# A hybrid decoder layer on one core: TensorE's unrolled recurrence heads written as a hardware loop

## The reference

```python
h = rms_norm(x, g_pre_mix)
z = h @ w_in                       # 16464 columns: q,k,v, indexer, HGRN q,f,i,g and two merge gates
o_a = sparse attention over the top-k keys
# HGRN2, 16 heads of 128 x 128
f = lb + (1 - lb) * sigmoid(hf);  k = 1 - f
b = cumsum(log f)                  # within a chunk
o = (q*exp(b)) @ S + causal((q exp(b)) . (k exp(-b))) @ v
S = exp(b_end) * S + (k * exp(b_end - b)).T @ v
o_b = rms_norm(o) * silu(hg)
x = x + rms_norm((sigmoid(ga)*o_a + sigmoid(gb)*o_b) @ w_out)
x = x + rms_norm(cross_attend(rms_norm(x), memory))
x = x + rms_norm(conv_ffn(rms_norm(x)))
```

## Time and profile before

| | us |
|---|---|
| median of 3 runs | 2759.55 |
| lowest, highest | 2756.3, 2761.29 |
| profiled execution, its own time | 2759.55 |
| its span, first to last instruction | 2758.0 |
| outside the span | 1.55 |
| a turn of two heads in the HGRN stage | 97.64 |

### The profile page before, as it was taken

The page is one execution under the profiler, slowest core; times in us unless marked ns, Lnnn a source line. Parts: engine busy times, 40 slices in busy tenths (PEclk is TensorE's granted clock), DMA queues, the critical chain, the costliest instruction groups (busy, mean ns, idle before and its releaser), DMA issues.

```text
span 2758.0 us, 49470 instructions
## 1 busy us (share of the span) xinstructions
PE 2693.2 (98%) x20086; PEld 2558.8 (93%) x20086; DVE 1605.0 (58%) x2399; ACT 1081.5 (39%) x1363; POOL 200.0 (7%) x293
## 2 busy tenths in 40 slices
PE   8999999999999999999989999999999999999998
PEld 7999787799999999999889969989999999999997
DVE  5564564376777768777446334475655555653334
ACT  5332444444444444444434234443322333333334
POOL 0103211011111111111000000000000000000000
PEclk9999999999999999999999999999999999999999
DMA  9646656765655555555464694555555555445554
GB/s 295 175 123 165 207 170 200 218 187 148 161 150 159 152 148 155 147 156 153 125 204 123 212 391 115 142 161 148 145 149 152 152 147 145 140 136 149 154 147 145
DMA packets 693458, 458.59 MB, mean 166 GB/s; under 512 B 13646, under 2 KB 661422, under 8 KB 687342
## 3 DMA queue, kind: packets, MB, share of 16 engines
q1 hardware_dynamic: 681008, 414.25, 52.9%
q0 software_dynamic: 8608, 28.06, 3.6%
q10 hardware_dynamic: 3712, 14.35, 1.4%
HBM read 429.91 MB, written 26.72 MB: 166 GB/s over the span
## 4 chain that ended last, share of the span: by engine, by line
PE 92%; DVE 4%; ACT 2%; DMA 1%; issue 1%; ACTq 0%; POOL 0%; POOLq 0%; DVEq 0%; SPq 0%
PE psum L595 20%; PE psum L600 20%; PE psum L597 20%; PE psum L840 4%; PE psum L1264 4%; PE psum L1265 4%; PE psum L1266 4%; PE psum L845 2%; PE psum L983 1%; PE psum L986 1%; PE psum L979 1%; PE psum L1144 1%; PE psum L701 1%; DMA ring<-in_w_in 1%; PE psum L995 1%
## 5 line engine op out<-in xcount | busy, mean ns | idle before, releaser
L595 PE MATMUL psum<-x_high,w_high 128*128 128x320 f32 x3808 | 1131.3, 312 | 4.2 <-ACT w_high L1987 4.0
L597 PE MATMUL psum<-h_low,w_high 128*128 128x320 f32 x3344 | 985.0, 309 | 0.0
L1311 DVE TENSOR_TENSOR w_low<-ring,w_high 128x2048 fp32r<-128x2048 f32 x292 | 676.2, 2316 | 321.7 <-ACT w_high L1987 321.3
L1987 ACT ACTIVATE w_high<-ring 128x2048 fp32r<-128x2048 f32 x294 | 561.8, 1912 | 724.7 <-PE psum L600 555.7
L595 PEld LDWEIGHTS psum<-x_high,w_high 128*128 128x128 f32 x3808 | 715.4, 188 | 9.3 <-ACT w_high L1987 4.8
L597 PEld LDWEIGHTS psum<-h_low,w_high 128*128 128x128 f32 x3344 | 629.0, 188 | 2.7 <-issue 1.0
L600 PE MATMUL psum<-x_high,w_low 128*128 128x320 f32 x3808 | 597.4, 309 | 0.0
L600 PEld LDWEIGHTS psum<-x_high,w_low 128*128 128x128 f32 x3808 | 568.5, 188 | 0.0
L1264 PE MATMUL psum<-y_high,w_down_high 128*128 128x320 f32 x704 | 217.8, 309 | 3.3 <-DVE w_low L1907 1.7
L1266 PE MATMUL psum<-y_high,w_low 128*128 128x320 f32 x704 | 216.3, 307 | 0.0
L1265 PE MATMUL psum<-y_low,w_down_high 128*128 128x320 f32 x704 | 216.2, 307 | 0.0
(11 more groups left out here) (425 smaller groups left out, 2838.9 us busy)
## 6 DMA issues: line engine op xcount, KB each, us to landing
ring<-in_w_in SPq DMA_DIRECT2D x128, 1024.0 KB, 5.8
ring<-in_w_up SPq DMA_DIRECT2D x88, 1024.0 KB, 5.7
ring<-in_w_down SPq DMA_DIRECT2D x64, 704.0 KB, 4.7
ring<-in_w_xk SPq DMA_DIRECT2D x16, 1024.0 KB, 6.1
ring<-in_w_xv SPq DMA_DIRECT2D x16, 1024.0 KB, 5.2
ring<-in_w_out SPq DMA_DIRECT2D x16, 1024.0 KB, 5.8
ring<-in_w_xq SPq DMA_DIRECT2D x16, 1024.0 KB, 5.9
ring<-in_w_xo SPq DMA_DIRECT2D x16, 1024.0 KB, 5.8
```

The lines of the kernel that those rows point to most:

```text
L595: mm(out, w_hi[:, j % 2, k, :], x_hi[:, k, :], start=k == 0, stop=False)
L597: mm(out, w_hi[:, j % 2, k, :], lo[:, k, :], start=False, stop=False)
L1311: V.tensor_tensor(w_lo[:, j], ring[:, j], w_hi[:, j % 2].bitcast(FP32), ALU.subtract).then_inc(N.slab_lo, 1)
L1987: F(w_hi[:, j % 2], ring[:, j], ACT.Copy).then_inc(N.slab_hi, 1)
```

## The change

On PE alone, the Python loop that wrote out seven pairs of heads becomes a hardware loop of seven turns. The last two heads stay written out.

```diff
             by_chunks(B_HG, 1, h_lo, lambda q: pe.wait_ge(rows_loaded[q], 32), lambda q: None)
-            for it in range(NHG // 2 - 1):
+            with pe.Fori(0, NHG // 2 - 1) as it:
                 head(it, 0)
                 head(it, 1)
             head(NHG // 2 - 1, 0)
             head(NHG // 2 - 1, 1, last_head=True)
```

## The result

The changed kernel takes 2790.7 us (median of 4 runs, 2786.5 to 2795.4) against 2758.3 us for the kernel before on the same chip. The ratio is 1.0114, with a 95% interval of 1.0095 to 1.0134. The prediction had the sign and the place right. It had the size wrong: it said 2771, and the time lies just above its range, in the rival "two misses at each jump".

What follows compares the result with a forecast made beforehand. The prediction took PE, busy in all of the stage, as the bound. It summed 2759.55 - 0 (copies removed) + 1.4 (register work) + 10.2 (six jumps) = 2771.2, said 2771, range 2757 to 2789.

Steps and rivals of the forecast that it cites:

- two misses at each jump: Rival at the loop's jumps: the top's block and the next both fetched, 28 to 46 us, 2789 to 2807; chance 0.17.
- PE bounds the stage, and a pause adds one for one: In the heads' stage PE is busy all 97.64 us of a turn, so any unfed moment adds to the end.
- Removing the copies is worth nothing: Dropping six of seven body copies on PE gains 0, as the 51 code packets held up nothing.
- Register work, 1.4 us: Register operations for turn-dependent waits in the loop's body: 0.1 us a head, 1.4 us in all, bounds 0 to 4.
- The rival that exposed it in full, 4 us: Rival in the loop's body: register work fully exposed, 4 us, with a miss of 1.9 us, 2775; no chance of its own.
- The first block is gone at each of the six jumps: At each jump back, the body's first block has left PE's instruction memory and must be fetched; size 10.2 us over six.
- 1.7 us a jump: Idle PE at each jump back: 4.1 us until PE is fed less 2.4 us of queued matmuls; 0 to 1.9 by bounds.
- No loss of clock: After a pause of 1.7 us at a jump PE keeps full clock; beyond about 2.9 it would add 3 us a jump.
- One miss a jump, 0.61, against two, 0.17: Likeliest case at the loop's jumps: one block fetched at each, 2762 to 2780, chance 0.61; fetching two had 0.17.
- The rival of a resident body: Rival at the jumps: the whole body stays in PE's instruction memory, only register work is left, 2761; chance 0.2.
- faster: Rival in the stage: fewer code fetches free DMA time for weight tiles, at most 3 us, giving 2757; chance 0.02.

Runs made afterwards that it cites:

- e5_hint_top: The changed kernel with a prefetch hint for the backward branch as the first instruction of each turn: 2760.7 us against 2757.9, ratio 1.0006.
- e2_half: The changed kernel with three loops of two turns in place of one of seven, the seventh pair written out: 2768.7 us against 2759.0, ratio 1.0031.
- e8: The kernel before, with four groups of four tiles in a turn of the FFN up loop (L1123), top at place 0 of a block: 2761.0 us, ratio 1.0006.
- e9: The kernel before, with four groups of four tiles in a turn of the FFN up loop, top at place 230 of a block: 2790.2 us, ratio 1.0111.
- e11_up5: The kernel before, with five groups of four tiles in a turn of the FFN up loop, top at place 0 of a block: 2763.6 us, ratio 1.0023.
- e4_slot239: The changed kernel with the loop's first instruction at place 239 of a block of 256: 2807.1 us against 2759.0, ratio 1.0165.
- e3_slot0: The changed kernel with the loop's first instruction at the first place of a block of 256: 2783.6 us against 2759.0, ratio 1.0079.

## Why the prediction was right or wrong, point by point

- *PE bounds the stage, and a pause adds one for one.* Right. The busy columns of DVE and ACT are as before, and pauses, restarts and clock make up the turns' growth.
- *Removing the copies is worth nothing.* Right (e5_hint_top: one copy, no miss, and the pace of before). It removed no fetches either: 67 packets came in the stage where 51 had the earlier trace rows.
- *Register work, 1.4 us.* It is nothing that can be seen: where e2_half has no jump, its pace is that of before. The rival that exposed it in full, 4 us, fell with it.
- *The first block is gone at each of the six jumps.* Right, and right that ten blocks would be needed. e8 and e9 now show why: eight stay, one of them fetched ahead. By the Trainium skill, Runtime: NRT & Kernel Launch, section Instruction fetch mechanics, PE holds 2048 instructions; the trace of e8_up4 agrees with eight blocks, but e11_up5 and e9_up4_slot230 (1972 and 1578 instructions) jump with a miss, so a body below 2048 is no safe sign.
- *1.7 us a jump.* This is the first term that was mis-sized. The fetch with its branch was put at 3.8 us. At the third and fifth jump that is what it took, 3.8 and 3.9 us, with pauses of 1.93 and 1.96. At the other four it took 4.8 to 4.9 us, with pauses of 2.9 to 3.0: there the block's packet waited behind POOL's store of a head's state (the table below), and the bounds from single DMAs allowed for no other traffic. The six first pauses are 15.6 us, not 10.2.
- *No loss of clock.* Wrong, a term put at nothing. The clock fell to 1.2 GHz behind four of six jumps, which cost 1.4 to 1.5 us each (a busy column of 99.67 where 98.14 stands without it). The reading of the earlier trace rows, a loss after 2.9 us and none after 1.6, does not carry over: the pauses ahead of the falls were 1.93, 2.87, 1.96 and 2.87 us, and none followed 3.00 and 2.94. In e2_half none followed 2.90. What decides it stays open. PE's work also starts again with a loss of about 0.25 us a pause, for which the sum had no term.
- *One miss a jump, 0.61, against two, 0.17.* This is the step that failed in kind: the sum took one missing block a jump, and two were missing. The row for it was read rightly (a code packet just as the stage's first tile began), and the choice between the two sides of the boundary was made the wrong way. The top lay some 40 instructions before a block's end: 19 matmuls of two instructions each and those of the sequencer came between the two pauses. The second pauses are small here, 2.5 us at four of the jumps and none at the other two, yet e4_slot239 shows the rival at full size: 48 us, above the 28 to 46 that it was given.
- *The rival of a resident body* fell; *faster* fell as well.

So of the 25.2 us in the span, 18.1 are pauses (15.6 and 2.5), and the rest is the lower clock, about 5.8, and the restarts, about 2.5. Together that is about 1 us over the span's growth; the stage began 1.6 us earlier in this execution. The forecast had 10.2 for the first pauses, 1.4 for register work and nothing for the rest. The median of all runs lies 6 us above the profiled one. More falls of the clock would do it, and the mean granted clocks fit: 0.993 in the shortest execution (2783.0 us), 0.991 in the profiled one, 0.987 in two of the three longest (2795.4 and 2796.2). Only the profiled one was looked into jump by jump.

Why the branch took 3.8 us at one jump and 4.9 at another, the changed kernel's own trace tells. The store is POOL's issue at L2621, 512 KB of a head's state; all times are in us, and the two middle columns count from the start of the branch.

| jump | branch | store issued | code packet starts | first pause | 1.2 GHz behind |
|---|---|---|---|---|---|
| 1 | 4.95 | -1.2 | 2.6 | 3.00 | no |
| 2 | 4.83 | -1.3 | 2.4 | 2.94 | no |
| 3 | 3.79 | -0.4 | 1.0 | 1.93 | yes |
| 4 | 4.82 | -1.3 | 2.5 | 2.87 | yes |
| 5 | 3.85 | -0.6 | 1.1 | 1.96 | yes |
| 6 | 4.82 | -1.3 | 2.4 | 2.87 | yes |

Where the store was issued early, its packets (queue q0) began 0.2 us behind the branch and soon filled all 16 DMA engines, and the code packet started when the last of them ended. Where it was issued later, the code packet was ahead of nearly all of them. DMA queues of 738.3 to 739.8 us (second jump, 0.5 to 2.0 us behind the branch), then of 840.1 to 841.6 us (the same stretch of the third):

```profile
q0 software_dynamic: 103, 0.41, 95.1%
```

```profile
q0 software_dynamic: 63, 0.26, 56.5%
q8 instruction: 1, 0.02, 5.7%
```

The 15 jumps of e2_half, e3_slot0 and e4_slot239 agree: nine with the early store took 4.8 to 4.9 us, and the six with the late one 3.4 to 4.3. No run moved the store, so this is read from traces and not tried. In e9_up4_slot230 there is no such store, but only 16 instructions of the last block are run before the branch; two code packets were under way at once at each jump, one of them for 2.0 to 2.3 us, and the branches took 4.6 to 5.1 us. In e11_up5, with 180 instructions there and one packet, they took 3.3 to 3.6.

## What to carry to other kernels

In these runs, rolling a long stretch of a bound engine into a loop was free only while the blocks that a turn touches, plus the one ahead, stayed in its instruction memory: count them from the top's place in a block, not from the size of the body. If they do not stay, give the backward branch a prefetch hint, and put the top early in a block, so that the second block is not late either. Look also at what the DMA engines carry at the jump: a store of 512 KB issued 1.2 us ahead of the branch went with branches longer by 1 us. Before forecasting such a change, look for the signs in a trace: code packets that repeat by turn, COMPARE_BRANCH of microseconds, and idle time "by issue" where the program has no wait.

## What the runs showed of the hardware that was not expected

The place of a loop's top within its block of 256 instructions is worth 23 us in 2800 here, with every instruction the same (e3, e4), and 29 us in another loop (e8, e9). A missing block delays PE's sequencer by 3.3 to 5.1 us, of which the queued matmuls hide about 2, and 1 us of the difference goes with a 512 KB store that has the DMA engines when the block is asked for. A prefetch hint takes 35 ns, works as well 98 us ahead as 17, and brings one block. And the code of the whole turn is fetched again when a single block too many is touched: 34 packets in four turns of e9_up4_slot230, ten in a turn of the changed kernel, not one a turn.
